# Closing block of a transformer kernel in three passes, and float32 sums for its second norm

## The chip, the cores and the metric
The kernel runs on all eight cores of one Trainium2 chip. Each core computes 1024 of the 8192 tokens (2 batches of 4096) and reads all weights; cores exchange nothing. The metric is the device time of the slowest core in microseconds, and the reported number is the median of the runs. TensorE (PE) multiplies, VectorE (DVE), ScalarE (ACT) and GpSimd (POOL) do the elementwise work, and SyncE (SP), ACT and POOL each can issue DMA transfers on a queue of their own.

## What is computed
```python
h = rmsnorm(x, g_mix)
proj = h @ w_in                                  # 2048 -> u | v | z, 1024 each
u, v = gelu(proj[:, :1024]), gelu(proj[:, 1024:2048])
out_a = spatial_gating(u, v, w_s, b_s, g_v)      # per chunk of 128 tokens
out_b = multiscale_pool(z, w_pool, pool_scale)
x = x + concat(out_a, out_b) @ w_out             # 2048 -> 2048
h = rmsnorm(x, g_ffn)                            # the second norm
x = x + square(relu(h @ w_up)) @ w_down          # 2048 -> 8192 -> 2048
return rmsnorm(x, g_final)                       # the final norm
```
`rmsnorm(x, g)` is x divided by the root of the mean of its squares over 2048 channels, times g.

## The kernel before
Channels lie on partitions and tokens in the free dimension, so 2048 channels are 16 tiles of 128 partitions by 1024 tokens (`XR(m)` is tile m of the residual, float32, in `xr_h` or `xr_mid`). A product has weights of 128x128 as the stationary operand and 512 tokens as the moving one. One "job" (`pe_job`) is the sum over 16 input tiles k for one output tile m: 32 matmuls for both halves of the tokens, or 16 for one half. Results go into six PSUM banks in rotation (`NRING`); banks 6 and 7 hold the statistics.

The norm's factor needs a sum over all channels, hence over partitions. It is made on TensorE: the squares of a tile in bfloat16 (`sqr`) are multiplied by a 128x128 matrix of ones and summed over the 16 tiles in bank 6 or 7. ACT then makes `rstd_bc`, the reciprocal root, by Ln and Exp.

Weights are float32 in HBM. POOL's queue loads them, cast to bfloat16, as slabs of two output tiles (1 MB of float32) into a ring of five slots (`ringall`, `issue_loads`); the load of slab n waits for the job that last used slab n-5.

Every engine's instructions are listed in program order with their dependences (`P.add`, `P.dma`), and an engine runs its list strictly in order, waiting on semaphores. So what stands where in each list is what sets the order; there is no planner.

The stages that matter here:

- Output projection (`wo_part`, `wo_evac`, `wo_norm`, from 212 us): 16 tiles m. For each, TensorE runs 32 matmuls (L664), DVE adds the input tile `xstage` (loaded by SP two tiles ahead, into the buffer that evacuation m-2 has freed, L626) to both halves (L671), ACT writes the scaled bfloat16 copy `h2T` (L682) and the squares (L685), and TensorE adds the squares' sums by two matmuls (L693, L694), which stand in its list behind a later tile's job (`pend`, `flush_one`). Those of tiles 14 and 15 come behind the first job of the up projection.
- Feed-forward in four blocks of 2048 hidden channels: 16 up jobs (reading `h2T`, results squared into `MIX`), then 16 down jobs with the residual added by DVE (L803, L805). The fourth block's down jobs are written apart, as the closing block.
- Closing block (L813 to L865): once for each half of 512 tokens, 16 jobs of 16 matmuls. After each job comes the statistic matmul of the tile before (L853), DVE adds the residual (L841), ACT squares (L847) and multiplies by g_final in place (L857). The second half loads all eight slabs of the block's w_down again. At the end of a half the last tile's statistic, Ln (L862) and Exp (L865) follow. `final_half_out` multiplies by `rstd_bc` on DVE (L819) and stores one tile of 128x512 from SP's queue (L821): for the first half one tile behind each job of the second, for the second half all 16 at the end.

Of the kernel before, what the change touches and what calls it, by code (L numbers as in the profile page):

```python
# [24 lines left out]
NFB = DFF // (FB * 128)  # L25

# [62 lines left out]
def build_program(debug=False):  # L89
# [23 lines left out]
    out_d = nc.dram_tensor("outT", [D, TOK], F32, kind="ExternalOutput").ap()  # L113
# [9 lines left out]
    def sb(name, shape, dt, off):  # L123
        return nc.alloc_sbuf_tensor_at(name, list(shape), dt, offset=off)
# [24 lines left out]
    wstg = sb("wstg", [128, KC // 4, 4, 512], F32, S0)  # L149
    ringall = sb("ringall", [128, 2 * NSLOT, KC, 128], BF16, R0)  # L150

    gv_t = calloc("gv_t", [128, 1024], F32, 4096)
    rtmp = sb("rtmp", [128, 2, 512], F32, C0)
    bs_t = calloc("bs_t", [128, 1024], F32, 4096)
    rstd_bc = calloc("rstd_bc", [128, TOK], F32, 4096)
    wpool = calloc("wpool", [128, 4, 2, 256], BF16, 4096)
    wsT = calloc("wsT", [128, 8, 128], BF16, 2048)
# [477 lines left out]
    pend = []  # L635
    rexp2 = [None, None]
# [40 lines left out]
    def wo_norm(m):  # L677
        while len(pend) > 1:
            flush_one()
        parts = [(0, 512, x1_e[0][m]), (512, 1024, x1_e[1][m])] if m == KC - 1 else [(0, 1024, x1_e[1][m])]  # L680
        for c0, c1, ev in parts:
            h2h[1][m] = P.add("act", lambda e, c0=c0, c1=c1: e.activation(out=h2T[:, m, c0:c1], in_=XR(m)[:, c0:c1], func=AF.Copy,  # L682
                                                                        scale=vecs[:, G_FFN + m:G_FFN + m + 1]), [ev, mix_tile_last[7], cst])
        s = m % 2
        sq = P.add("act", lambda e: e.activation(out=sqr[:, s, :], in_=XR(m)[:, :], func=AF.Square), [x1_e[1][m], hs_reader[2 * s + 1]])  # L685

        def mk():
            d = [sq, ones_op]
# [65 lines left out]
    for fb in range(NFB):  # L754
        act_ops = [None] * FB
        lastblk = fb == NFB - 1
        for f in range(FB):
# [17 lines left out]
            for half in range(2):  # L775
# [4 lines left out]
                    [job, r2[0], rt_readers[s], vh_ops[7]])  # L780
# [32 lines left out]
    fb = NFB - 1  # L813
    pre_ops = [[None] * KC, [None] * KC]
    rexp = [None, None]

    def final_half_out(k, half):
        c0, c1 = half * 512, (half + 1) * 512
        o = P.add("dve", lambda e: e.tensor_tensor(out=XR(k)[:, c0:c1], in0=XR(k)[:, c0:c1], in1=rstd_bc[:, c0:c1], op=ALU.mult),  # L819
                  [rexp[half], pre_ops[half][k]])  # L820
        P.dma("sp", lambda e: e.dma_start(out=out_d[k * 128:(k + 1) * 128, c0:c1], in_=XR(k)[:, c0:c1]), "st", [o])  # L821

    for half in range(2):
        c0, c1 = half * 512, (half + 1) * 512
        pending = [None]
        last_mm = None
        for m in range(KC):
            n, mmi = nbase + fb * 16 + 8 + half * 8 + m // 2, m % 2
            if mmi == 0:
                issue_loads(n + NSLOT - 1)  # L830
            if half == 0 and m == 0:
                segs = [([(0, 0, 512, RS(n, k, mmi * 128, (mmi + 1) * 128), MIX(k)[:, c0:c1], k == 0, k == FB - 1)], [slab_ld[n], act_ops[k]])
                        for k in range(FB)]
            else:
                segs = [([(0, 0, 512, RS(n, k, mmi * 128, (mmi + 1) * 128), MIX(k)[:, c0:c1], k == 0, k == FB - 1) for k in range(FB)],
                         [slab_ld[n], act_ops[FB - 1]])]
            job, banks = pe_job(segs, nb=1)
            slab_done[n] = job
            if pending[0] is not None:
                last_mm = pending[0]()  # L840
            ev = P.add("dve", lambda e, m=m, b=banks[0], c0=c0, c1=c1: e.tensor_tensor(out=XR(m)[:, c0:c1], in0=XR(m)[:, c0:c1], in1=ps[:, b, :], op=ALU.add),  # L841
                       [job, x2_ops[m], x2_e1[m], h2_ops[m]])
            bank_last[banks[0]] = ev
            hsl = hs_ctr[0] % 4
            hs_ctr[0] += 1
            sq_ap = sqr[:, hsl // 2, (hsl % 2) * 512:(hsl % 2) * 512 + 512]
            sq = P.add("act", lambda e, m=m, sq_ap=sq_ap, c0=c0, c1=c1: e.activation(out=sq_ap, in_=XR(m)[:, c0:c1], func=AF.Square), [ev, hs_reader[hsl]])  # L847

            def mk(m=m, sq=sq, sq_ap=sq_ap, hsl=hsl, half=half):
                d = [sq, ones_op]  # L850
                if m == 0:
                    d.append(bank_last[6 + half])
                pe = P.add("pe", lambda e: e.matmul(ps[:, 6 + half, :], ones[:, :], sq_ap, start=(m == 0), stop=(m == KC - 1)), d)  # L853
                hs_reader[hsl] = pe
                return pe
            pending[0] = mk
            pre_ops[half][m] = P.add("act", lambda e, m=m, c0=c0, c1=c1: e.activation(out=XR(m)[:, c0:c1], in_=XR(m)[:, c0:c1], func=AF.Copy,  # L857
                                                                                      scale=vecs[:, G_FIN + m:G_FIN + m + 1]), [ev, sq, cst])
            if half == 1:
                final_half_out(m, 0)  # L860
        last_mm = pending[0]()
        ln = P.add("act", lambda e, half=half, c0=c0, c1=c1: e.activation(out=rstd_bc[:, c0:c1], in_=ps[:, 6 + half, :], func=AF.Ln, bias=EPSB, scale=1.0 / D),  # L862
                   [last_mm, eps_op, last_rstd_reader[0]])
        bank_last[6 + half] = ln
        rexp[half] = P.add("act", lambda e, c0=c0, c1=c1: e.activation(out=rstd_bc[:, c0:c1], in_=rstd_bc[:, c0:c1], func=AF.Exp, scale=-0.5), [ln])  # L865
    for k in range(KC):
        final_half_out(k, 1)

    keys = P.finalize()
    with ExitStack() as es:  # L870
# [19 lines left out]
        @block.sync  # L890
        def _(e):
            P.emit("sp", e, sems)
            e.wait_ge(sems["dma_st"], P.dma_counts["dma_st"])
    return nc
# [60 lines left out]
```

How the kernel before makes its waits and increments, by code:

```python
    def emit(self, eng, e, sems):  # L72
        waited = {}
        for op in self.ops[eng]:
            for d in op.deps:
                if d.kind == "c" and d.eng == eng and eng in ("pe", "sp"):
                    continue
                assert d.val is not None
                if waited.get(d.semkey, 0) >= d.val:
                    continue
                e.wait_ge(sems[d.semkey], d.val)
                waited[d.semkey] = d.val
            ins = op.fn(e)
            if op.kind == "d":
                ins.then_inc(sems[op.semkey], 16)
            elif op.signal:
                ins.then_inc(sems[eng], 1)
# [802 lines left out]
        @block.sync  # L890
        def _(e):
            P.emit("sp", e, sems)
            e.wait_ge(sems["dma_st"], P.dma_counts["dma_st"])
```

## Time and profile before

| | us |
|---|---|
| median of 3 runs (lowest, highest) | 1246.85 (1245.58, 1465.36) |
| profiled run, its time | 1246.34 |
| profiled run, span of its slowest core (core 7) | 1244.8 |
| spans of the eight cores in it | 1238.2 to 1244.8 |

The highest of the three is a run in which a die ran at a lower clock. The page of the profile and all rows are of core 7 in the profiled run. Times are microseconds from the span's start unless marked ns. A record of a matmul lasts from its start until its result is drained, so neighbours overlap; what counts in a stream is the distance from start to start.

### The profile page before, as it was taken

How to read it: one execution, taken by the hardware profiler on the slowest of the kernel's cores; microseconds unless marked ns; L12 is line 12 of the kernel's file. 1: busy time of each engine (PE TensorE's matmuls, PEld its weight loads, DVE VectorE, ACT ScalarE, POOL GpSimd, SP SyncE). 2: the span in 40 equal slices, each digit the busy share in tenths (PEclk: the TensorE clock that was granted, in tenths of full speed). 3: DMA queues.
4: the chain of work that ended last, by engine and by line, in shares of the span. 5: the costliest groups of instructions: out<-in, count | busy, mean ns of one | idle time of the engine just before them, and what ended most of it. 6: DMA issues, size and time to landing. Idle time of an engine off the chain costs nothing.

```text
span 1244.8 us, 14345 instructions; the slowest of 8 cores (1238.2 to 1244.8 us)
## 1 busy us (share of the span) xinstructions
PE 1202.4 (97%) x5736; PEld 547.2 (44%) x5736; DVE 334.8 (27%) x551; ACT 230.6 (19%) x443; POOL 82.0 (7%) x113
## 2 busy tenths in 40 slices
PE   4899999999999999999999999999999999999993
PEld 2354444444444444444444444444444444444441
DVE  3466556321122121212111111111111111121234
ACT  2401155133321100001110000111100011123332
POOL 0100022100000000000000000000000000001000
PEclk9999999999999999999999999999999999999997
DMA  8994530987534443444345433443454335458875
GB/s 277 232 173 76 85 77 2 160 176 156 118 68 70 86 81 69 69 88 80 68 70 88 80 68 71 88 79 68 70 90 77 68 69 94 76 93 144 147 158 169
DMA packets 37921, 126.95 MB, mean 102 GB/s; under 512 B 2784, under 2 KB 2912, under 8 KB 36832
## 3 DMA queue, kind: packets, MB, share of 16 engines
q0 software_dynamic: 24912, 95.43, 45.1%
q1 hardware_dynamic: 12944, 30.61, 7.7%
q8 instruction: 47, 0.77, 0.2%
q14 instruction: 18, 0.15, 0.0%
HBM read 213.05 MB, written 8.39 MB: 178 GB/s over the span
## 4 chain that ended last, share of the span: by engine, by line
PE 93%; DMA 4%; DVE 1%; SPq 1%; ACT 0%; issue 0%; DVEq 0%; ACTq 0%
PE ps L219 83%; PE ps L664 7%; DMA xf<-xT 2%; DMA xstage<-xT 2%; PE ps L407 1%; PE ps L853 1%; SPq L237 0%; PE ps L319 0%; DVE xr_h L819 0%; DVE xr_mid L819 0%; PE ps L541 0%; PE ps L358 0%; PE ps L693 0%; PE ps L694 0%; SPq L241 0%
## 5 line engine op out<-in xcount | busy, mean ns | idle before, releaser
L219 PE MATMUL ps<-h2T,ringall 128*128 128x512 bf16 x2048 | 442.8, 379 | 0.0
L219 PEld LDWEIGHTS ps<-h2T,ringall 128*128 128x128 bf16 x2048 | 200.4, 98 | 241.6
L219 PE MATMUL ps<-pooled,ringall 128*128 128x512 bf16 x1024 | 234.1, 379 | 0.0
L219 PE MATMUL ps<-uT,ringall 128*128 128x512 bf16 x1024 | 234.1, 379 | 0.0
L778 DVE SCALAR_TENSOR_TENSOR rtmp<-ps,rstd_bc 128x512 f32<-128x512 f32 x128 | 82.4, 686 | 360.9 <-PE ps L219 350.0
L219 PEld LDWEIGHTS ps<-pooled,ringall 128*128 128x128 bf16 x1024 | 100.2, 98 | 120.8
L219 PEld LDWEIGHTS ps<-uT,ringall 128*128 128x128 bf16 x1024 | 100.1, 98 | 120.7
L783 ACT ACTIVATE uT<-rtmp 128x512 bf16<-128x512 f32 x64 | 39.1, 631 | 504.6 <-DVE rtmp L778 504.4
L219 PE MATMUL ps<-hT,ringall 128*128 128x512 bf16 x384 | 83.7, 379 | 0.0
L783 ACT ACTIVATE pooled<-rtmp 128x512 bf16<-128x512 f32 x64 | 39.3, 631 | 181.7 <-DVE rtmp L778 181.7
L284 POOL DMA_DIRECT2D ringall<-w_down x40 | 28.6, 714 | 454.1 <-PE ps L219 379.9
L219 PEld LDWEIGHTS ps<-hT,ringall 128*128 128x128 bf16 x384 | 37.3, 98 | 44.4
L219 PE MATMUL ps<-ringall,hT 128*128 128x512 bf16 x256 | 56.2, 379 | 0.0
L803 DVE TENSOR_TENSOR xr_mid<-xr_mid,ps 128x512 f32<-128x512 f32 x24 | 16.5, 687 | 134.9 <-PE ps L219 134.9
L803 DVE TENSOR_TENSOR xr_h<-xr_h,ps 128x512 f32<-128x512 f32 x24 | 16.5, 687 | 134.9 <-PE ps L219 134.9
L284 POOL DMA_DIRECT2D ringall<-w_up x32 | 22.8, 713 | 425.9 <-PE ps L219 340.5
L664 PE MATMUL ps<-uT,ringall 128*128 128x512 bf16 x224 | 50.6, 379 | 0.2 <-DVE uT L549 0.2
L664 PE MATMUL ps<-pooled,ringall 128*128 128x512 bf16 x224 | 50.6, 379 | 0.0
L407 PE MATMUL ps<-hT,ringall 128*128 128x512 bf16 x128 | 37.0, 416 | 0.8 <-ACT hT L386 0.8
L219 PEld LDWEIGHTS ps<-ringall,hT 128*128 128x128 bf16 x256 | 24.8, 98 | 29.0
L664 PEld LDWEIGHTS ps<-uT,ringall 128*128 128x128 bf16 x224 | 21.8, 98 | 26.9 <-issue 0.7
L664 PEld LDWEIGHTS ps<-pooled,ringall 128*128 128x128 bf16 x224 | 21.8, 98 | 26.0 <-issue 0.2
(103 smaller groups left out, 541.5 us busy)
## 6 DMA issues: line engine op xcount, KB each, us to landing
ringall<-w_down POOLq DMA_DIRECT2D x40, 1024.0 KB, 9.5
ringall<-w_up POOLq DMA_DIRECT2D x32, 1024.0 KB, 9.5
ringall<-w_in POOLq DMA_DIRECT2D x10, 1024.0 KB, 11.6
xf<-xT SPq DMA_DIRECT2D x8, 1024.0 KB, 19.7
xstage<-xT SPq DMA_DIRECT2D x16, 512.0 KB, 10.5
ringall<-w_out POOLq DMA_DIRECT2D x7, 1024.0 KB, 16.9
wstg<-w_in SPq DMA_DIRECT2D x4, 1024.0 KB, 15.8
outT<-xr_h SPq DMA_DIRECT2D x16, 256.0 KB, 3.9
```

Of the source, the lines that this page charges most:

```text
L219: ins = e.matmul(ps[:, banks[sel], c0:c1], lhsT, rhs, start=st, stop=sp_)
L284: slab_ld[n] = P.dma("pool", lambda e, n=n: e.dma_start(out=ringall[:, 2 * (n % NSLOT):2 * (n % NSLOT) + 2, :, :], in_=slabs[n]), "slot%d" ...
L407: ins = e.matmul(ps[:, z_banks[half][m], :], ringall[:, m, k, :], hT[:, k, half * 512:(half + 1) * 512], start=(k == 0), stop=(k == KC - 1))
L664: ins = e.matmul(ps[:, banks[half], :], wo_w(m, k), MIX(k)[:, half * 512:(half + 1) * 512], start=(k == K_POOL[0]), stop=(k == K_GATE[-1]))
L778: a1 = P.add("dve", lambda e, s=s, half=half, b=banks[half]: e.scalar_tensor_tensor(out=rtmp[:, s, :], in0=ps[:, b, :], scalar=0.0, in1=rs ...
L783: a2 = P.add("act", lambda e, s=s, f=f, half=half: e.activation(out=MIX(f)[:, half * 512:(half + 1) * 512], in_=rtmp[:, s, :], func=AF.Squ ...
L803: e1 = P.add("dve", lambda e, m=m, b=banks[0]: e.tensor_tensor(out=XR(m)[:, 0:512], in0=XR(m)[:, 0:512], in1=ps[:, b, :], op=ALU.add), [jo ...
L853: pe = P.add("pe", lambda e: e.matmul(ps[:, 6 + half, :], ones[:, :], sq_ap, start=(m == 0), stop=(m == KC - 1)), d)
```

## The change
The output projection: squares of tile 0 go as float32 into `sqacc`, those of tiles 1 to 13 into the one buffer `sqf`, and DVE adds `sqf` to `sqacc`, one tile behind (`accumulate`). After tile 13 DVE splits the sum into two bfloat16 parts, high and low, which TensorE multiplies by the ones (4 matmuls). Tiles 14 and 15 keep direct squares (`sq_end`) and two matmuls each.

The closing block: `PASSES` are tokens 0 to 512, 512 to 768 and 768 to 1024. The weights are loaded once: ten tiles stay in the ring's five slots and six go into `wres`, in the place of `h2T`, with loads that wait for the last up job. The tiles of passes 0 and 1 are multiplied by g_final and `rstd_bc` in one DVE operation and stored from SP during the next pass. The last pass keeps ACT's product with g_final. At its end DVE multiplies 12 tiles and POOL 4, in groups of 1, 1, 2, 4, 4 and of 2, 2, into `ostage`; DVE reads the reciprocal root from PSUM, POOL from SBUF, for which Exp runs twice. The groups are stored from SP's and ACT's queues in seven transfers. The output tensor has a new shape, 128 partitions of 16384 floats, which the host puts in order.

```diff
+PASSES = ((0, 512), (512, 768), (768, 1024))
+NRES = 6
-    out_d = nc.dram_tensor("outT", [D, TOK], F32, kind="ExternalOutput").ap()
+    out_d = nc.dram_tensor("outT", [128, KC * TOK], F32, kind="ExternalOutput").ap()
...
-        for j in range(8):
+        for j in range(8 if fb < NFB - 1 else NSLOT):
             slabs.append(w_down_d[:, 16 * fb + 2 * j:16 * fb + 2 * j + 2, :, :])
-    for j in range(8):
-        slabs.append(w_down_d[:, 16 * (NFB - 1) + 2 * j:16 * (NFB - 1) + 2 * j + 2, :, :])
...
+        if sq_wait:
+            accumulate(sq_wait.pop())
+        first, direct = m == 0, m >= SQ_DIRECT          # SQ_DIRECT = KC - 2
+        dst = sqacc if first else sq_end[m - SQ_DIRECT] if direct else sqf
+        sq = P.add("act", lambda e: e.activation(out=dst[:, :], in_=XR(m)[:, :], func=AF.Square), [x1_e[1][m], acc_last[0]])
...
+    def accumulate(item):
+        m, sq = item
+        acc_last[0] = P.add("dve", lambda e: e.tensor_tensor(out=sqacc[:, :], in0=sqacc[:, :], in1=sqf[:, :], op=ALU.add), [sq, acc_last[0]])
+        if m == SQ_DIRECT - 1:
+            hi = P.add("dve", lambda e: e.tensor_copy(out=sqr[:, 0, :], in_=sqacc[:, :]), [acc_last[0]] + hs_reader)
+            lo = P.add("dve", lambda e: e.tensor_tensor(out=sqr[:, 1, :], in0=sqacc[:, :], in1=sqr[:, 0, :], op=ALU.subtract), [hi])
...
+    issue_loads(NSLAB - 1)
+    up_last = slab_done[nlast - 1]
+    for j in range(NRES // 2):
+        t0 = 16 * NFB - NRES + 2 * j
+        wres_ld.append(P.dma("pool", lambda e, j=j, t0=t0: e.dma_start(out=wres[:, 2 * j:2 * j + 2, :, :], in_=w_down_d[:, t0:t0 + 2, :, :]),
+                             "wres%d" % j, [up_last]))
...
+    def final_out(i, k):
+        t0, t1 = PASSES[i]
+        o = P.add("dve", lambda e: e.scalar_tensor_tensor(out=XR(k)[:, t0:t1], in0=XR(k)[:, t0:t1], scalar=vecs[:, G_FIN + k:G_FIN + k + 1],
+                                                          in1=rstd_bc[:, t0:t1], op0=ALU.mult, op1=ALU.mult), [rexp[i], x3_ops[i][k], cst])
+        P.dma("sp", lambda e: e.dma_start(out=out_block(i, k, 1), in_=XR(k)[:, t0:t1]), "st", [o])
+    for i, (t0, t1) in enumerate(PASSES):
...
+            if i > 0:
+                final_out(i - 1, m)
...
+    for eng, m0, n in (("dve", 0, 1), ("dve", 1, 1), ("pool", lo0, 2), ("dve", 2, 2), ("dve", 4, 4), ("pool", lo0 + 2, 2), ("dve", 8, 4)):
+        rs = rps if eng == "dve" else rstd_bc[:, t0:t1]
+        tail_ops[m0] = (n, P.add(eng, lambda e, m0=m0, n=n, rs=rs: e.tensor_tensor(
+            out=ostage[:, m0:m0 + n, :], in0=xr_group(m0, n), in1=rs.unsqueeze(1).broadcast_to([128, n, T]), op=ALU.mult),
+            [exp_ps if eng == "dve" else rexp[-1], pre_ops[m0 + n - 1], last_job]))
+    for queue, sem, starts in (("sp", "st", (0, 2, 8)), ("act", "sta", (1, lo0, 4, lo0 + 2))):
+        for m0 in starts:
+            n, o = tail_ops[m0]
+            P.dma(queue, lambda e, m0=m0, n=n: e.dma_start(out=out_block(len(PASSES) - 1, m0, n), in_=ostage[:, m0:m0 + n, :]), sem, [o])
```

## Rows read from the trace of the kernel before

**Rows 1.** The page: its span, and the chain that ended last by engine

```profile
span 1244.8 us, 14345 instructions; the slowest of 8 cores (1238.2 to 1244.8 us)
...
PE 93%; DMA 4%; DVE 1%; SPq 1%; ACT 0%; issue 0%; DVEq 0%; ACTq 0%
```

**Rows 2.** Windows: window, length, busy us (instructions) by engine, PEclk, DMA share, GB/s

```profile
205.00:258.00 53.00, 51.81 (x258) 23.99 (x257) 20.67 (x42) 14.96 (x44) 8.24 (x10) 1.00 0.71 126
...
331.00:1105.30 774.30, 774.30 (x3590) 351.00 (x3588) 143.87 (x224) 83.28 (x134) 39.97 (x56) 1.00 0.44 77
...
1165.70:1224.30 58.60, 58.60 (x272) 26.45 (x271) 19.36 (x31) 21.99 (x33) 2.14 (x3) 1.00 0.65 139
```

**Rows 3.** The same view, a stretch within the output projection

```profile
250.00:255.00 5.00, 5.00 (x25) 2.24 (x23) 1.29 (x2) 0.18 (x1) 0.00 (x0) 1.00 1.00 186
```

**Rows 4.** Timeline (start, length, instruction): statistics at both halves' ends, first product

```profile
1163.55 0.38 PE L853 MATMUL ps<-sqr,ones 128*128 128x512 bf16 x1
...
1165.50 0.38 PE L853 MATMUL ps<-sqr,ones 128*128 128x512 bf16 x1 [1.57 <-ACT sqr L847]
...
1224.01 0.38 PE L853 MATMUL ps<-sqr,ones 128*128 128x512 bf16 x1
...
1227.96 2.49 DVE L819 TENSOR_TENSOR xr_h<-xr_h,rstd_bc 128x512 f32<-128x512 f32 x4 [2.39 <-ACT rstd_bc L865]
```

**Rows 5.** Transfers: two windows and the stores of the end; the first 35 us

```profile
1232.00:1238.00 6.00, 0.00 (x0) 0.00 (x0) 5.68 (x10) 0.00 (x0) 0.00 (x0) 0.50 1.08 287
1238.00:1241.00 3.00, 0.00 (x0) 0.00 (x0) 0.00 (x0) 0.00 (x0) 0.00 (x0) 0.50 1.06 368
...
L821 SPq DMA_DIRECT2D outT<-xr_h x8: 332/560/977, 1228.7 to 1238.7; - x8
...
DMA to landing us min/median/max: 2.9/5.0/5.9
...
DMA packets 3296, 9.93 MB, mean 284 GB/s; under 512 B 444, under 2 KB 572, under 8 KB 2620
```

**Rows 6.** Chain by time (start, us): matmuls of 16 and 128 columns, two projection tiles

```profile
75.77 0.79 PE ps L358 x32
...
186.12 0.45 PE ps L541 x8
...
301.68 6.91 PE ps L664 x32
309.02 6.91 PE ps L664 x32
```

**Rows 7.** Timeline of the output projection's first half, PE and DVE

```profile
233.92 0.38 PE L693 MATMUL ps<-sqr,ones 128*128 128x512 bf16 x1
...
253.43 1.29 DVE L671 TENSOR_TENSOR xr_h<-ps,xstage 128x512 f32<-128x512 f32 x2 [8.16 <-DMA xstage<-xT]
...
257.06 0.38 PE L693 MATMUL ps<-sqr,ones 128*128 128x512 bf16 x1 [0.96 <-ACT sqr L685]
...
260.14 1.29 DVE L671 TENSOR_TENSOR xr_mid<-ps,xstage 128x512 f32<-128x512 f32 x2 [5.42 <-DMA xstage<-xT]
```

**Rows 8.** Groups by form (busy us, mean ns of one): durations used for new operations

```profile
L841 DVE TENSOR_TENSOR xr_h<-xr_h,ps 128x512 f32<-128x512 f32 x16 | 11.0, 687 | 44.1 <-PE ps L219 44.1
...
L847 ACT ACTIVATE sqr<-xr_h 128x512 bf16<-128x512 f32 x16 | 10.1, 631 | 35.7 <-DVE xr_h L841 35.7
...
L603 ACT ACTIVATE sqv<-vf 128x128 f32<-128x128 f32 x64 | 18.8, 299 | 0.4
...
L433 DVE TENSOR_TENSOR tmpA<-zE 128x1039 f32<-128x1039 f32 x8 | 9.9, 1232 | 0.1
...
L605 POOL TENSOR_SCALAR vrs<-vstat 128x8 f32<-128x8 f32 x8 | 2.5, 318 | 50.5 <-ACT sqv L603 50.5
...
L446 DVE TENSOR_TENSOR ptmp<-tmpA,invc 128x16 f32<-128x16 f32 x4 | 0.7, 175 | 0.4
...
L415 DVE TENSOR_TENSOR sqh<-xh 128x256 bf16<-128x256 f32 x1 | 0.4, 418 | 0.0
```

More of the change, by code:

```diff
@@ new lines, in stat_sum, with fn, mk @@
+    def stat_sum(parts, start, stop, deps):
+        def fn(e):
+            ins = None
+            for i, p in enumerate(parts):
+                for half in range(2):
+                    ins = e.matmul(ps[:, 6 + half, :], ones[:, :], p[:, half * 512:(half + 1) * 512], start=start and i == 0, stop=stop)
+            return ins
+        return P.add("pe", fn, deps)
+    def accumulate(item):
[4 more added lines that the diff above has]
+            lo = P.add("dve", lambda e: e.tensor_tensor(out=sqr[:, 1, :], in0=sqacc[:, :], in1=sqr[:, 0, :], op=ALU.subtract), [hi])
+            def mk():
+                pe = stat_sum([sqr[:, 0, :], sqr[:, 1, :]], True, False, [hi, lo, ones_op, bank_last[6], bank_last[7]])
+                hs_reader[:] = [pe] * 4
+                return pe, m
+            pend.append(mk)
@@ L811, in build_program @@
         prev_down_last = dj
[L813 to L824, printed above, removed]
+    nlast = nbase + (NFB - 1) * 16 + 8
@@ L850, in mk @@
+            sq = P.add("act", lambda e, m=m, sq_ap=sq_ap, t0=t0, t1=t1: e.activation(out=sq_ap, in_=XR(m)[:, t0:t1], func=AF.Square), [ev, hs_reader[hsl]])
+            def mk(m=m, sq=sq, sq_ap=sq_ap, hsl=hsl, T=T, sbank=sbank):
                 d = [sq, ones_op]
                 if m == 0:
-                    d.append(bank_last[6 + half])
-                pe = P.add("pe", lambda e: e.matmul(ps[:, 6 + half, :], ones[:, :], sq_ap, start=(m == 0), stop=(m == KC - 1)), d)
+                    d.append(bank_last[sbank])
+                pe = P.add("pe", lambda e: e.matmul(ps[:, sbank, 0:T], ones[:, :], sq_ap, start=(m == 0), stop=(m == KC - 1)), d)
@@ L856, in build_program @@
             pending[0] = mk
[L857 to L860, printed above, removed]
+            if lastp:
+                pre_ops[m] = P.add("act", lambda e, m=m, t0=t0, t1=t1: e.activation(out=XR(m)[:, t0:t1], in_=XR(m)[:, t0:t1], func=AF.Copy,
+                                                                                    scale=vecs[:, G_FIN + m:G_FIN + m + 1]), [ev, sq, cst])
@@ L865, in build_program @@
-        rexp[half] = P.add("act", lambda e, c0=c0, c1=c1: e.activation(out=rstd_bc[:, c0:c1], in_=rstd_bc[:, c0:c1], func=AF.Exp, scale=-0.5), [ln])
-    for k in range(KC):
-        final_half_out(k, 1)
+        bank_last[sbank] = ln
+        if lastp:
+            rps = ps[:, 7, 0:T]
+            exp_ps = P.add("act", lambda e, t0=t0, t1=t1: e.activation(out=rps, in_=rstd_bc[:, t0:t1], func=AF.Exp, scale=-0.5), [ln, bank_last[7]])
+        rexp[i] = P.add("act", lambda e, t0=t0, t1=t1: e.activation(out=rstd_bc[:, t0:t1], in_=rstd_bc[:, t0:t1], func=AF.Exp, scale=-0.5), [ln])
@@ L952 @@
         b, q = divmod(c, 4)
-        out[b, q * TOK:(q + 1) * TOK, :] = np.asarray(res.results[c]["outT"], np.float32).T
+        o = np.asarray(res.results[c]["outT"], np.float32)
+        for t0, t1 in PASSES:
+            blk = o[:, KC * t0:KC * t1].reshape(128, KC, t1 - t0)
+            out[b, q * TOK + t0:q * TOK + t1, :] = blk.transpose(2, 1, 0).reshape(t1 - t0, D)
     return out
```

80 lines of the change are left out of this document (48 added, 32 removed).

## The prediction

> **What bounds the kernel now.** I read the shares of the chain that ended last first: 93% of the 1244.8 us span are TensorE's [rows 1]. Then the stages in windows [rows 2]. In the feed-forward stages (331 to 1105 us) TensorE has no idle time at a granted clock of 1.00, the 2.4 GHz level, and the same holds in the second half of the closing block. Shortening anything there pays only if it takes matmuls out of TensorE's queue. Two stretches differ. One is the first half of the output projection (205 to 258 us), where TensorE idles 1.19 us [rows 2] while the DMA engines are full [rows 3]. The other is the end: the last projection matmuls end near 1224.0, and the span ends at 1244.8. These 20.8 us hold a short chain of ACT and DVE work and then stores [rows 4, 5]. The change touches exactly these: the statistic matmuls of the output projection, the closing block and the end.
>
> **Part A, the second norm's sums.** Before, each of 16 tiles costs two 512-column matmuls with the ones (L693, L694), 32 in all. Matmuls start 6.91/32 = 0.216 us apart [rows 6], and from the tile at 301.68 to that at 309.02 the period is 7.34 us: 32 projection matmuls (6.91) and one pair (0.43) [rows 6]. After, the split sum takes 4 matmuls and tiles 14 and 15 take 2 each: 8 in all. 24 x 0.216 = 5.2 us leave TensorE's queue, and nothing takes their place: the pairs that are left sit after tile 15 and after the first up tile.
> The new work lies on DVE and ACT. Thirteen float32 additions of 1024 columns (nearest row 1.23 us, L433), a cast and a subtraction (1.23 each at most) [rows 8] add 1.3 us per 6.9 us tile to the 1.3 of the two evacuations. ACT's next square waits for the addition, and that ends about as ACT's own scaled copy of the tile does (1024 columns, twice a 512-column row of 0.63 at most). I cost this at nothing; its cover is TensorE's 6.9 us tile, of which some 4 us stay free. If that cover failed, a tile would cost at most the 1.23 us of one addition more. The addition stands in DVE's queue ahead of later evacuations, hence of freed banks, but those come a tile later.
> One stall also goes. The pair of tile 3 waited 0.96 us for its square, because the input tile for it had landed only at 253.4 [rows 7]. What is late next: six banks in pairs, so job m needs the evacuation of m-3. Without pairs and stall, jobs 3, 4, 5 run from 233.92 to 254.65 (3 x 6.91), and job 6 needs evacuation 3, over at 254.72 [rows 7]: a start near 254.8 instead of 257.5, right behind the pair at 257.06. Job 7 is then ready at 261.7, and evacuation 4 is over at 260.14 + 1.29 = 261.4. That is 0.3 us of room; later tiles have 3 us. So the stall is worth 0.96 - 0.15 = 0.8 us, and A is 5.2 + 0.8, taken as 5.9 us. The lower bound is the case in which nothing is gained ahead of job 6, because the DMA engines set its time (share 1.00 from 250 to 255 [rows 3]): after job 6 there were 24 of the 32 matmuls and now 8, so 16 x 0.216 = 3.45 us. The upper bound is 6.1.
>
> **Part B, the closing block.** Pass 0 is the former first half, with the same matmuls. Passes 1 and 2 have 2 x 272 matmuls of 256 columns, where the second half had 272 of 512. No row has 256 columns. Spacings are 0.79/32 = 25 ns at 16 columns, 0.45/8 = 56 at 128 and 216 at 512 [rows 6]; all three with their own weight load, whose record lasts 98 ns (0.10 us in the timelines). Were it not hidden, 207 ns each would cost 53 us; at 25 and 56 ns it is hidden. They lie on columns/2.4 plus 2.5 ns down to 128 columns, so 256 columns cost 109 ns; bounds are 108 (half of 216) and 112 (twice 56). 542 x 0.109 = 59.2 against 271 x 0.216 = 58.5: +0.7 us, bounds 0.0 to 2.2.
> As a check on this, the Trainium skill, "TensorE: Matmul & The Clock Gate", section on the back-to-back issue gap, gives sustained spacings of 81 ns at 128 and 131 ns at 512 columns with a weight load each. The trace disagrees on both (56 and 216). An estimate between its figures would be 98 ns at 256 columns, 5 to 6 us less for the block than my sum; I go by the rows.
> There is one more pass boundary. At the present one, statistic 15 starts 1.95 us after statistic 14 (1163.55 to 1165.50): drain, evacuation, square [rows 4]. With 256 columns the evacuation goes from 0.69 to 0.42 us and the square from 0.63 to 0.41 (between the rows of 128 and 512 columns, and a DVE row of 256, L415 [rows 8]): 1.95 - 0.49 = 1.46 us, say 1.4. The rest of it, some 1.3 us beyond the matmul itself, is new idle time, bounds 1.0 to 1.9. Within a pass, the same chain of 1.4 us must fit under one job of 16 x 0.109 = 1.75 us, and does. On DVE evacuation and the previous pass's final multiplication take 0.35 + 0.61 of 1.86 us. That is cover, but thin: if the chain grew by 0.4 us, each further 0.1 us would cost 3.2 us over 32 tiles.
> Weights are loaded once: 5 slots and 3 loads into the dead h2T, 8 loads instead of the 16 of the code before. On POOL's queue the last four stand behind the last up tile and nothing waits behind them. The first is needed 8 x 3.67 = 29 us later; 4.2 MB at the 186 GB/s of a full stretch [rows 3] take 23. I cost it at nothing (if it were late, up to 3 us once). The two-operand final multiplication replaces an ACT copy and a DVE product, off the path. SP issues 32 stores in the passes, one in 1.86 us, where one takes 0.33 [rows 5]. B: -0.7 - 1.4 - 0.2 for a shorter cover at the first job of each pass = -2.3 us, range -1.0 to -4.
>
> **Part C, the end.** Before, from 1224.01 to DVE's first product at 1227.96 there are 3.95 us [rows 4]. With 256 columns: evacuation -0.27, square -0.22, statistic -0.11, Ln -0.22, Exp -0.22: about -1.0 us.
> From the first product (call it D) to the end there were 16.8 us [rows 4]. DVE made 256 KB in 0.61 us, 430 GB/s, and the DMA engines were full (share 1.08 and 1.06) at 287 and 368 GB/s [rows 5]. So stores set this end. The two full windows together give (6 x 287 + 3 x 368)/9 = 314 GB/s; 4.19 MB take 13.3 us at that, and the other 3.5 us are the first product and issue ahead and the landing behind. After, only 2.10 MB are left: 6.7 us, and the first product is 0.35 us shorter. Does the supply keep up? DVE: 0.33, 0.33, 0.60, 1.14, 1.14 = 3.6 us for 12 tiles (PSUM as an operand costs the same: 0.69 us in L841 [rows 8]; four products from SBUF alone take 3 x 0.61 + 0.68 = 2.5 [rows 4]). POOL multiplies 4 tiles in two operations that no row shows; the same shape on DVE takes 0.69, and POOL's smallest operation takes 318 ns where a small one on DVE takes 175 (L446) [rows 8], 1.8 times, so 0.7 to 1.24 us each. All is supplied by D+3.8, while DMA needs until about D+8. So D+6.7+3.5-0.35 = D+9.9, and at the 368 GB/s of the better window D+8.8. I take 9.6, since two of seven groups are twice and two four times as wide as a store before, so -7.2 us. Issues on ACT have no row; SP's took 0.33 to 0.98, and four in 3 us fit. C: 8.2 us; bounds 3.8 (below) and 9.0 (368 GB/s all the time).
>
> **Sum.** 5.9 - 2.3 + 8.2 = 11.8 us. Span 1244.8 - 11.8 = 1233.0; the profiled run took 1.5 us more than its span (1246.34), and the median 1246.85 lies 0.5 above that: 1235.
>
> **Rivals.**
> Input tiles set the projection. The weight load now issued at 254 instead of 256.65 competes with input tile 4; A falls to 3.45 and the time is 1237.5. For it: DMA is full there. Against: the 3 us of room from tile 5 on.
> The end is bound by supply and landing. DVE and POOL hold each other up in SBUF, so the products last 3.6 + 2.5 = 6.1 us, and the last 512 KB land like the slowest 256 KB did (5.9 us [rows 5]) plus 2: D+14, a gain of 2.8 instead of 7.2: 1239.4. Against: DVE's rstd now comes from PSUM.
> Stores in the new layout are slow (the other side). The output now has partitions 64 KB apart, in pieces of 1 to 4 KB, instead of rows 4 KB apart. Ahead of D 4.6 us are saved, so the end may take 21.4 us; less 3.2 that is 2.10 MB in 18.2 us: below 115 GB/s the kernel gets slower. At 100 it takes 21 us for them, 1250, and more with the backlog of pass 1. Against: loads of xT have the same 64 KB step, and the opening moved 9.93 MB at 284 GB/s with them [rows 5]. Beside it, the Trainium skill, "DMA: Bandwidth & Descriptors", section on latency and other measured facts, reports copies between tensors in HBM falling from 207 to 103 GB/s as the partitions' step grows from 512 KB to 4 MB. No run here shows it.
> Narrow matmuls run closer than 109 ns. If what spaces them were the weight load's 98 ns, 542 x 0.011 = 6.0 us less: 1229. The straight line through three rows speaks against.
> The change doesn't shorten TensorE's queue, the pairs of statistics being free already: then A is 0.8 and the time 1240. The 7.34 us period speaks against.
>
> **Chances.** Forecast 0.62; input tiles 0.13; supply and landing 0.14; slow stores 0.03; closer matmuls 0.04; statistics free 0.02; else 0.02. The range 1230 to 1242 takes in the first three and the bounds of B, with two rivals together. About 2% (25 us) is what a measurement of this kernel can tell from no change: faster than that 0.02, within it 0.94, slower 0.04 (slow stores far below 100 GB/s, or the thin cover in the narrow passes gone).
>
> **What the profile would show.** Right: the tile period in the projection is 6.91 instead of 7.34 and there are 8 statistic matmuls there; 16 matmuls of 256 columns take 1.75 us; two idle gaps of 1.6 and 1.3 us in the closing block; 8 loads of w_down in it; the end from the last projection matmul takes 12 to 13 us (2.95 + 9.6) instead of 20.8, with DMA share near 1 for most of it. Wrong: TensorE idle at each tile of a narrow pass; a bank wait of over 1 us at jobs 6 to 9; stores under 200 GB/s at the end; POOL's products over 2 us.

## The result, and the profile after

| | before | after |
|---|---|---|
| median (lowest, highest), us | 1247.06 (1245.58, 1465.36), 4 runs | 1236.84 (1234.72, 1238.04), 4 runs |
| profiled run, us | 1246.34 | 1238.04 |
| its span, slowest core | 1244.8 (core 7) | 1236.2 (core 0) |
| spans of all cores | 1238.2 to 1244.8 | 1229.5 to 1236.2 |

The execution of 1465.36 had one die at a lower clock; the ratios, and the medians in the sections below, leave such executions out. The ratio is 0.9917, with an interval from 0.9903 to 0.9931: some 10 us faster, well inside 2%, against a forecast of 1235. The total came out close; on the slowest cores two of its three terms did not, and their errors cancel. The page of the kernel after, its span, transfers and chain by engine (before: [rows 1]):

```profile
span 1236.2 us, 14873 instructions; the slowest of 8 cores (1229.5 to 1236.2 us)
...
DMA packets 36755, 118.59 MB, mean 96 GB/s; under 512 B 2768, under 2 KB 5200, under 8 KB 35664
...
PE 92%; DMA 5%; DVE 1%; issue 1%; SPq 1%; ACT 0%; DVEq 0%; ACTq 0%
```

DMA's share of the chain rose from 4% to 5% although the end, where the stores stand, got shorter. Two waits for input tiles stand in the output projection. The first, for tile 3, was in the chain before too, with 21.84 us; the second, for tile 5, is new. This is the chain in order of time (start, length, step), kernel after:

```profile
231.50 22.28 DMA xstage<-xT
255.23 15.59 DMA xstage<-xT
```

**Where the time went.** Four marks split the span. The end of the projection is read at the start of the second up job, since all statistics of the second norm stand ahead of it. The other marks are the statistic of tile 14 in pass 0, the one of tile 14 in the last pass, and the first product of the end, D.

| us, slowest core | before | after | change | forecast |
|---|---|---|---|---|
| second up job starts (A) | 338.64 | 337.92 | -0.7 | -5.9 |
| statistic 14, pass 0 | 1163.55 | 1162.83 | -0.7 | |
| from there to statistic 14, last pass (B) | 60.46 | 62.64 | +2.2 | +2.3 |
| statistic 14 to D (C) | 3.95 | 2.82 | -1.1 | -1.0 |
| D to the end (C) | 16.84 | 7.91 | -8.9 | -7.2 |
| span | 1244.8 | 1236.2 | -8.6 | -11.8 |

These are marks of core 7 before and of core 0 after. On average over the eight cores of the same two traces the span fell by 9.0 us: A gave 2.7, B cost 2.2, and C gave 1.1 and 7.3 (from D to the end 15.4 before, 8.1 after). Core 7 had the longest end of the eight before (14.7 to 16.8 us). So C's gain beyond the forecast is one of the slowest cores; on average only A missed.

The closing block and the end, timeline of the kernel after (start, length, instruction, idle time before it):

```profile
1162.83 0.38 PE L896 MATMUL ps<-sqr,ones 128*128 128x512 bf16 x1
...
1164.78 0.38 PE L896 MATMUL ps<-sqr,ones 128*128 128x512 bf16 x1 [1.57 <-ACT sqr L890]
...
1194.47 0.27 PE L896 MATMUL ps<-sqr,ones 128*128 128x256 bf16 x1
...
1195.87 0.27 PE L896 MATMUL ps<-sqr,ones 128*128 128x256 bf16 x1 [1.13 <-ACT sqr L890]
...
1225.47 0.27 PE L896 MATMUL ps<-sqr,ones 128*128 128x256 bf16 x1
...
1228.29 1.35 DVE L925 TENSOR_TENSOR ostage<-xr_h,ps 128x256 f32<-128x256 f32 x3 [1.74 <-ACT ps L911]
1228.74 2.48 POOL L925 TENSOR_TENSOR ostage<-xr_h,rstd_bc 128x512 f32<-128x512 f32 x2 [120.60 <-ACT rstd_bc L912]
```

The wide boundary is the old one (1.95 us, as in [rows 4]); the narrow one takes 1.40. Windows inside the two narrow passes, and in the last stores (columns as in [rows 2]):

```profile
1164.90:1194.40 29.50, 29.50 (x271) 26.43 (x271) 16.34 (x30) 7.58 (x17) 0.00 (x0) 1.00 0.34 126
1195.90:1225.40 29.50, 29.50 (x271) 26.42 (x272) 12.24 (x30) 14.71 (x32) 0.00 (x0) 1.00 0.21 72
...
1230.00:1233.00 3.00, 0.00 (x0) 0.00 (x0) 1.90 (x2) 0.00 (x0) 1.22 (x1) 0.50 0.98 366
```

TensorE has no idle time in either pass: the thin cover held. The stores flow at 366 GB/s, where the old end had windows of 287 and 368 [rows 5].

**Why A gave so little here.** The projection of the kernel after on core 0, timeline:

```profile
255.31 3.61 PE L672 MATMUL ps<-pooled,ringall 128*128 128x512 bf16 x16 [0.51 <-DVE xr_h L679]
255.35 0.72 POOL L289 DMA_DIRECT2D ringall<-w_out  x1 [23.45 <-PE ps L672]
...
261.77 1.29 DVE L679 TENSOR_TENSOR xr_mid<-ps,xstage 128x512 f32<-128x512 f32 x2 [5.48 <-DMA xstage<-xT]
...
263.21 3.61 PE L672 MATMUL ps<-pooled,ringall 128*128 128x512 bf16 x15 [0.83 <-DVE xr_mid L679]
...
270.91 1.29 DVE L679 TENSOR_TENSOR xr_mid<-ps,xstage 128x512 f32<-128x512 f32 x2 [6.72 <-DMA xstage<-xT]
...
272.35 2.97 PE L672 MATMUL ps<-pooled,ringall 128*128 128x512 bf16 x7 [2.07 <-DVE xr_mid L679]
```

Jobs 6, 7 and 8 each wait for a freed bank: 0.51, 0.83 and 2.07 us, together 3.41. The evacuations that free the banks wait for input tiles. Tile 5's load was issued at 255.23, the load of 1 MB of w_out at 255.35, and the tile took 15.59 us to land, to 270.8. In the kernel before, the same two marks are these (core 7):

```profile
256.65 0.71 POOL L284 DMA_DIRECT2D ringall<-w_out  x1 [24.75 <-PE ps L664]
...
263.87 1.29 DVE L671 TENSOR_TENSOR xr_mid<-ps,xstage 128x512 f32<-128x512 f32 x2 [2.43 <-DMA xstage<-xT]
```

There the weight load was issued at 256.65, and evacuation 5 began at 263.87, not 270.91. What follows the third wait, in windows of the same core:

```profile
270.00:272.00 2.00, 0.27 (x2) 0.00 (x0) 1.09 (x2) 0.00 (x0) 0.72 (x1) 1.00 0.17 62
272.00:274.00 2.00, 1.65 (x5) 0.72 (x6) 2.00 (x4) 1.71 (x2) 0.00 (x0) 0.64 0.21 20
274.00:276.00 2.00, 2.00 (x7) 0.64 (x5) 1.76 (x2) 1.66 (x3) 0.00 (x0) 0.51 0.95 168
276.00:278.00 2.00, 2.00 (x11) 0.94 (x10) 0.00 (x0) 1.03 (x1) 0.00 (x0) 1.00 1.01 161
```

The granted clock fell to the 1.2 GHz level (7 matmuls in 2 us where 9 or 10 fit) and came back. That costs 0.36 x 2 + 0.49 x 2 = 1.7 us. So 3.4 + 1.7 = 5.1 us of A's 5.9 are taken back on this core. The others waited less: over the eight cores, the second up job starts at 336.87 on average before and at 334.16 after, 2.7 us earlier.

That start also holds what came before the projection. The projection's first matmul is at 208.18 to 211.92 us on the eight cores before and at 210.03 to 212.13 after. From there to the second up job the stage takes 126.46 us on average before and 123.03 after, 3.4 less. The four kernels under "The end" leave this stage alone, and in their traces it takes 121.8 to 122.4 on average, 4.1 to 4.6 less. So A's yield differs from execution to execution, and that of the profiled one here is the lowest of these five.

### The profile page after: what moved, and what is told of

Read it like the earlier page. It is cut to its first block, busy times and chain, and to the rows that moved or that the text cites. A ratio compares the mean times of both kernels' runs of the same rounds, so it can differ in the third digit from the quotient of the medians.

```text
span 1236.2 us, 14873 instructions; the slowest of 8 cores (1229.5 to 1236.2 us)
## 1 busy us (share of the span) xinstructions
PE 1193.5 (97%) x5880; PEld 571.5 (46%) x5984; DVE 354.9 (29%) x587; ACT 221.0 (18%) x446; POOL 78.8 (6%) x107
## 4 chain that ended last, share of the span: by engine, by line
PE 92%; DMA 5%; DVE 1%; issue 1%; SPq 1%; ACT 0%; DVEq 0%; ACTq 0%
PE ps L226 83%; PE ps L672 6%; DMA xstage<-xT 3%; DMA xf<-xT 2%; PE ps L412 1%; PE ps L896 1%; SPq L244 0%; PE ps L324 0%; PE ps L546 0%; DVE ostage L925 0%; PE ps L363 0%; SPq L248 0%; DVE xr_h L679 0%; PE ps L709 0%; DVE xr_h L883 0%
## 5 line engine op out<-in xcount | busy, mean ns | idle before, releaser
L226 PE MATMUL ps<-pooled,ringall 128*128 128x512 bf16 (+1 forms) x989 | 212.1, 362 | 1.0
L226 PE MATMUL ps<-uT,ringall 128*128 128x512 bf16 (+1 forms) x992 | 212.1, 362 | 0.8
L226 PE MATMUL ps<-hT,ringall 128*128 128x512 bf16 x375 | 82.6, 379 | 0.6 <-issue 0.2
L672 PE MATMUL ps<-pooled,ringall 128*128 128x512 bf16 x218 | 51.7, 388 | 3.7 <-DVE xr_mid L679 2.9
L672 PE MATMUL ps<-uT,ringall 128*128 128x512 bf16 x220 | 50.4, 379 | 0.4 <-DVE uT L554 0.2
L289 POOL DMA_DIRECT2D ringall<-w_down x29 | 20.7, 714 | 379.9 <-PE ps L226 379.9
L412 PE MATMUL ps<-hT,ringall 128*128 128x512 bf16 x125 | 35.4, 409 | 0.8 <-ACT hT L391 0.8
```

Of the source, the lines that this page charges most:

```text
L226: ins = e.matmul(ps[:, banks[sel], c0:c1], lhsT, rhs, start=st, stop=sp_)
L289: slab_ld[n] = P.dma("pool", lambda e, n=n: e.dma_start(out=ringall[:, 2 * (n % NSLOT):2 * (n % NSLOT) + 2, :, :], in_=slabs[n]), "slot%d" ...
L412: ins = e.matmul(ps[:, z_banks[half][m], :], ringall[:, m, k, :], hT[:, k, half * 512:(half + 1) * 512], start=(k == 0), stop=(k == KC - 1))
L672: ins = e.matmul(ps[:, banks[half], :], wo_w(m, k), MIX(k)[:, half * 512:(half + 1) * 512], start=(k == K_POOL[0]), stop=(k == K_GATE[-1]))
```

## The experiments

Theory 1 throughout: the new sums take 5.2 us out of TensorE's queue, as forecast, but the stage then asks for input tiles earlier, beside a weight load that is issued earlier too, and the tiles come late; the end is a matter of store bytes and their rate. Its rivals stand in the expectations. Where these speak of the "last statistic" of the projection: in kernels with the new sums it is one row of four matmuls, 0.87 us ahead of the second up job, in the others a row of one, 0.21 ahead. That makes the new sums look 0.66 us better than they are, so I compare starts of the second up job ("U", all eight cores). U includes where the projection began, which differs by up to 4 us between the cores of a trace; where that matters I give the stage's length, from its first matmul to U.

### The two halves of the change alone

The first kernel is the one before with `accumulate`, `sq_end` and the split sum, the second is the one after with pairs of statistics for each tile again:

```diff
 # sums only, on the kernel before
-        s = m % 2
-        sq = P.add("act", ... out=sqr[:, s, :] ...)        # two matmuls per tile
+        first, direct = m == 0, m >= SQ_DIRECT
+        dst = sqacc if first else sq_end[m - SQ_DIRECT] if direct else sqf
 # block only, on the kernel after: the same lines the other way round
```

> The kernel before with only the new sums of the second norm's squares (part A); closing block and output as before. Theory 1 (the sums take 24 matmuls out of TensorE's queue, but the output projection is then held by its input tiles: they still arrive from full DMA queues, and jobs 6, 7 and 8 wait for freed banks): the start of the up projection moves 2 to 3 us earlier in the mean of the cores and about 1 us on the slowest; time 1243.5 to 1246, ratio 0.997 to 0.999; bank waits of 1 to 4 us per core between 250 and 275 us. Theory 2 (the forecast: TensorE alone sets the projection): 5 to 6 us less, time near 1241, ratio 0.995, bank waits under 0.5 us.

> The changed kernel with the old sums of the second norm (parts B and C alone). Theory 1 (the end gained 10 us on the slowest core, the block lost 2.2, and part A gave little): time 1238.5 to 1240, ratio 0.993 to 0.995; from the first product to the end about 8 us. Theory 2 (part A gave its 5 us and the end only about 8): time near 1241, ratio 0.9955.

Sums only: 1243.65 us (from 1241.10 to 1248.39) beside 1246.26, ratio 0.9983 (0.9967 to 0.9999). U is 334.63 on average (329.7 to 338.1), 2.2 us better than before. Waits of TensorE on core 6 (total, times, longest):

```profile
PE ps L670 <- DVE xr_mid L677: 3.1, 1, 3.1
PE ps L877 <- ACT sqr L871: 3.1, 2, 1.6
PE ps L670 <- DVE xr_h L677: 1.0, 1, 1.0
```

The bank waits are there without the block: they come with the new sums. Block only: 1241.34, ratio 0.9956 (0.9939 to 0.9972), where 1238.5 to 1240 was expected. Its last stage does what theory 1 says: D to the end takes 7.81 to 8.18 us on all cores. But U is 338.10 on average (335.4 to 342.1), 1.2 us later than before, for work that is the same in both. The stage began no later (210.4 on average in both), so the 1.2 us are inside it. The waits of its core 7, the slowest (total, times, longest):

```profile
PE ps L695 <- ACT sqr L687: 3.0, 1, 3.0
```

Input tile 4 took 17.23 us to land there, its square came 2.98 us late for the statistic matmuls at 266.18, and the granted clock then fell as above (0.91 from 262 to 280 us). So tiles can come late with the old sums too; TensorE then waits for a square and not for a bank. The longest such wait in the kernel before was 1.61 us, on core 4. This stage moves by a microsecond or two between kernels with the same instructions in it.

### Weight loads held back

`issue_loads` makes a slab's load wait for an input tile as well:

```diff
+    late_for = {17: 5, 18: 7}     # slab: input tile
 ...
+            if n in late_for:
+                deps.append(xs_ld[late_for[n]])
```

> The changed kernel with two waits more on POOL's queue: the w_out loads of tiles 12, 13 and of 14, 15 start only when input tiles 5 and 7 have landed; they are needed 30 us later. Theory 1 (the moved-up w_out load shares the DMA engines with input tiles 4, 5, 6, and that makes jobs 6 to 8 wait; on two cores the wait of 2.1 us also drops TensorE's clock to 1.2 GHz for 4 us): waits of TensorE between 250 and 275 us fall under 1 us per core, granted clock 1.00 in the stage on all cores, time 2 to 4 us below the changed kernel, 1232.5 to 1235. Theory 2 (the input tiles are late for another reason, their own double buffer and the four earlier weight loads): waits stay, time as the changed kernel, 1236 to 1237.

> The changed kernel with the w_out loads of tiles 8 to 15 issued one by one, each after an input tile has landed (after tiles 3, 4, 6 and 8), so that input tiles 2 to 6 meet at most one weight load. Theory 1 (input tiles late because DMA is shared with five weight loads): input tile 2 is added before 240 instead of 245.5, no bank waits, TensorE without idle time from 230 to 330 us; time 3 to 5 us below the changed kernel, 1231.5 to 1234. Theory 2 (TensorE's queue is not what the projection waits for, or the delayed weights come late themselves): no gain, or new waits of TensorE for w_out loads; 1236 or more.

The second kernel has {15: 3, 16: 4, 17: 6, 18: 8} and also lists these four loads one by one, with tiles 3, 4, 6 and 7, so that each can wait for its own input tile. With the first, no core waits for a bank between 250 and 275 us, the clock stays at 1.00 there, and U is 329.2 to 331.8 on six cores. Their stage takes 120.2 to 120.4 us, some 6 less than before. That is the forecast of A, by an edit that touches only when weights are loaded: the cause is shown. Yet the time is 1237.23, ratio 0.9931 (0.9916 to 0.9945), no better than after, where 1232.5 to 1235 was expected. Two cores have a new wait; core 0 of it, timeline:

```profile
321.82 1.29 DVE L682 TENSOR_TENSOR xr_h<-ps,xstage 128x512 f32<-128x512 f32 x2 [5.68 <-DMA xstage<-xT]
323.03 1.21 DVE L718 TENSOR_TENSOR sqacc<-sqacc,sqf 128x1024 f32<-128x1024 f32 x1
324.35 0.69 DVE L720 CAST sqr<-sqacc 128x1024 bf16<-128x1024 f32 x1
325.14 1.23 DVE L721 TENSOR_TENSOR sqr<-sqacc,sqr 128x1024 bf16<-128x1024 f32 x1
...
326.52 1.39 PE L712 MATMUL ps<-sqr,ones 128*128 128x512 bf16 x4 [4.03 <-DVE sqr L721]
```

Input tile 14 landed at 321.8. The loads behind the delayed ones had bunched up (DMA share 0.96 from 284 to 320 us); that this made it late is what the next experiment tries. The addition, cast and subtraction stand behind its evacuation in DVE's queue, and the four matmuls stand ahead of the whole up projection: 4.0 us idle, and U is 336.8 there. The granted clock falls here too (0.76 from 326 to 333 us), which takes another 1.7 us. With {15: 3, ...} it is the same at other cores: no bank waits, 3.2 and 5.0 us at the split sum on cores 1 and 5, 1237.17 us, ratio 0.9917 (0.9893 to 0.9942), where 1231.5 to 1234 was expected. The gain was made and given back 60 us later.

### All weight loads of the stage held back

```diff
-    late_for = {17: 5, 18: 7}
+    late_for = {17: 5, 18: 7, 19: 9, 20: 11, 21: 13, 22: 15}
 # and, in the second kernel, the split sum's matmuls behind the first up job
-        while len(pend) > 1:
+        while len(pend) > 1 and m < KC - 1:
```

> The changed kernel with the two delayed w_out loads of e3_late_weights and also the four w_up loads of the projection held back, each until input tile 9, 11, 13 or 15 has landed (they are needed 13 to 50 us later). Theory 1 (the whole projection runs close to what the DMA engines can bring, some 18 MB in 110 us at 180 GB/s, and which input tile is late depends on what shares the engines with it): no TensorE wait over 1 us on any core, neither at 250 to 275 nor at 320 to 330, all cores end the stage within 3 us; time 1231 to 1234. Theory 2 (the late tiles 13 and 14 of two cores in e3_late_weights come from the delay of the two w_out loads, so more delay is worse): waits of 3 us and more at the end of the stage, or TensorE waits for w_up in the first up jobs; 1236 or more.

> As e5_all_late, and the four matmuls of the split sum stand behind the first up job instead of ahead of it. Theory 1 (in TensorE's queue they wait for DVE's evacuation of tile 14, hence for input tile 14, and block an up job that could run): on cores where tile 14 is late the 3 to 5 us of waiting in front of the up job shrink to under 1.5 us; where it isn't late nothing changes; time 1231 to 1233, with less spread than e5_all_late. Theory 2 (the up job needs the tile too, so the wait only moves into it): as e5_all_late within 0.5 us.

1232.21 us beside 1245.55, ratio 0.9888 (0.9873 to 0.9903). U is 331.42 on average (329.1 to 333.1): 5.5 us ahead of before, although the stage began 0.6 us later. Its length is 120.43 on average, 6.0 less than before, where the forecast for A was 5.9, and 120.2 to 120.6 on all eight cores. Core 1 of it, the last of the eight there, its waits in that stage (a single one), and one window over the stage:

```profile
PE ps L675 <- DVE uT L558: 0.2, 1, 0.2
```

```profile
205.00:330.00 125.00, 124.76 (x603) 57.34 (x601) 53.40 (x81) 42.07 (x69) 11.81 (x15) 1.00 0.71 146
```

0.24 us idle in 125, clock 1.00. The stage is bound by TensorE's queue alone, and moving as many bytes as before (DMA share 0.71) was never the obstacle; their order was. The second kernel gives 1232.37, the same ratio: with no tile late, the place of the four matmuls decides nothing, so this run doesn't settle what it would be worth in the kernels above.

The same six waits on the kernel before:

> The kernel before with nothing but the held-back weight loads of e5_all_late (two of w_out, four of w_up). Theory 1 (the old sums leave TensorE 5.2 us more to do in the projection, so its input tiles were hardly late; only the wait of 0.3 to 2.1 us for a square goes): 0.5 to 2 us less, ratio 0.9985 to 0.9995, and the last statistic of the stage at 335.5 to 337 on all cores. Theory 2 (holding back the weights is a gain of its own, whatever the sums): 4 us less, ratio near 0.9965.

1242.56 beside 1243.52, ratio 0.9992 (0.9981 to 1.0002), U 334.94 on average (333.5 to 337.0, where 335.5 to 337 was expected for the statistic 0.2 us ahead of it). By the time it is worth nothing that can be told; of the 1.9 us in U, 1.2 are an earlier start of the stage. The late weights pay because the sums shortened the stage, not by themselves. The stage's length shows it: on average 126.46 us before, 124.11 with the sums alone, 125.74 with the late loads alone and 120.43 with both (the kernel above), that is 2.3 and 0.7 us for each and 6.0 together. The last core's U says the same: 339.15, 338.14, 337.02 and 333.09.

### The end

All stores from SP; one transfer a tile; the output tensor in its former shape:

```diff
-    for queue, sem, starts in (("sp", "st", (0, 2, 8)), ("act", "sta", (1, lo0, 4, lo0 + 2))):
+    for queue, sem, starts in (("sp", "st", (0, 1, 2, lo0, 4, lo0 + 2, 8)),):        # one queue
-            P.dma(queue, ... out_block(..., m0, n), in_=ostage[:, m0:m0 + n, :])
+            for j in range(n):                                                        # single tiles
+                P.dma(queue, ... out_block(..., m0 + j, 1), in_=ostage[:, m0 + j:m0 + j + 1, :])
-        return out_d[:, KC * t0 + k0 * (t1 - t0):KC * t0 + (k0 + nk) * (t1 - t0)]
+        return out_d[:, k0:k0 + nk, t0:t1]                                            # old layout
```

> The changed kernel with the seven last stores all issued from SP. Theory 1 (the end was shortened by halving what is left to store; 2.1 MB at 375 GB/s keep the DMA engines full for 5.6 of its 7.9 us, and seven issues of 0.33 us fit on one queue): from the first product to the end 7.7 to 8.3 us, as before. Theory 2 (the second queue feeds the engines better than one): 9 to 10 us.

> The changed kernel with the 16 tiles of the last pass stored one by one (pieces of 1 KB for each partition instead of up to 4 KB), from the same two queues behind the same products. Theory 1 (wide pieces raised the store rate from 314 to 375 GB/s): from the first product to the end 9 to 9.8 us, rate near 300 GB/s with the engines full. Theory 2 (width does not matter; the rate of before was low because half as wide a window of queues or the cores' shares set it): 7.7 to 8.3 us.

> The changed kernel with the old output tensor (a partition's rows 4 KB apart), passes and groups kept; a group's transfer then has pieces of 1 KB. Theory 1 (the width of pieces matters, the distance of partitions does not): as t2_single_tiles, 9 to 9.8 us from the first product to the end. Theory 2 (the new 64 KB distance costs something): below t2_single_tiles, 8 us. Theory 3 (neither matters): 7.7 to 8.3 us in both.

These are single executions, so I read D to the end on all eight cores and not the totals (1236.48, 1235.79 and 1238.56 us).

| | D to the end, us | GB/s, D + 1.7 to D + 4.7 |
|---|---|---|
| after | 7.91 to 8.40 | 365 to 370 |
| one queue | 7.74 to 7.94 | 363 to 370 |
| single tiles | 8.44 to 8.59 | 318 to 320 |
| old layout | 8.58 to 8.82 | 312 to 314 |

The same window of single tiles and of one queue:

```profile
1227.30:1230.30 3.00, 0.00 (x0) 0.00 (x0) 1.98 (x2) 0.00 (x0) 1.31 (x2) 0.50 0.95 318
```

```profile
1228.90:1231.90 3.00, 0.00 (x0) 0.00 (x0) 1.87 (x2) 0.00 (x0) 1.20 (x1) 0.50 0.98 369
```

The second queue is worth nothing. The Trainium skill, "DMA: Bandwidth & Descriptors", in its rules for kernel authors, says that spreading transfers over several issuing engines gives no bandwidth, since all use the same 16 DMA engines; the trace agrees (363 to 370 GB/s either way). The length of the contiguous piece is what the new layout brings: with 1 KB to a partition in each piece, in either layout, 312 to 320 GB/s; with up to 4 KB 365 to 370. It is worth 0.5 us here, less than I expected (9 to 9.8 us for single tiles), and the 64 KB from partition to partition cost nothing.

Passes of 512, 320 and 192:

```diff
-PASSES = ((0, 512), (512, 768), (768, 1024))
+PASSES = ((0, 512), (512, 832), (832, 1024))
```

> The changed kernel with passes of 512, 320 and 192 tokens. Theory 1 (the end is 2.3 us fixed plus bytes at 375 GB/s, and a job of 192 columns, 16 x 0.0825 = 1.32 us, still covers the chain of evacuation and square, about 1.25): 16 jobs of the last pass in 22.4 us without idle time between them, from the first product to the end 6.5 us instead of 7.9, time 1.5 to 2 us below the changed kernel. Theory 2 (the chain no longer fits under the job): TensorE waits 0.1 to 0.3 us at each statistic, 1.6 to 4.8 us in all, and the gain at the end is lost.

D to the end takes 6.45 to 6.55 us, 1.4 less than after, and statistic 14 to D 2.57 instead of 2.82. The window at the end has the same rate on fewer bytes:

```profile
1226.50:1229.50 3.00, 0.00 (x0) 0.00 (x0) 1.12 (x2) 0.00 (x0) 0.65 (x1) 0.50 1.00 364
```

1.57 MB at 364 GB/s are 4.3 us, and 2.2 us lie around them, as after (2.10 MB at 367 are 5.7, of 7.9). A tile's period is 1.40 us in the last pass, with no wait inside it. So the step is worth 1.6 us by its parts. The stretch from U to the end of the span shows them: 896.8 to 896.9 us on its eight cores, 898.2 to 898.8 in the kernel after. The total doesn't show it: 1237.35 us (from 1233.25 to 1240.81), ratio 0.9949 (0.9929 to 0.9969). Its profiled run was the fastest of all, 1233.25; its projection still has the bank waits (U from 329.4 to 334.6), which differ from execution to execution. The others have no trace. In the two slowest of them the last core's span is 1238.9 and 1237.1 us, where the next core's is 1234.1 and 1232.8: a delay of single cores, as the waits of the projection are, but the reason is argued and not shown.

### Everything together

All six late loads, the split sum behind the first up job, and passes of 512, 320, 192:

> e6_sum_behind_up joined with the passes of 512, 320 and 192 tokens. Theory 1 (both gains are in different places and add): 1.5 to 2 us below e6_sum_behind_up, time 1230 to 1231.5, ratio 0.987 to 0.988, with the small spread of e6_sum_behind_up. Theory 2 (the wide spread of t4_last_192 came from its narrower pass and not from the projection): spread of several us here too and no gain.

1229.83 us (from 1229.73) beside 1243.52, ratio 0.9888 (0.9868 to 0.9908), where 0.987 to 0.988 was expected, and spans from 1226.2 to 1227.9: the fastest version, and better than both kernels. No core waits in the projection (U 329.2 to 331.2), and D to the end is 6.46 to 6.88. Against the late loads without the 192 columns the ratio is the same, but the kernel before was 2 us faster on this chip, so the times leave open what the 192 columns add. The traces tell: from U to the end of the span are 896.7 to 897.2 us here and 898.2 to 899.0 in the two kernels with all late loads, on every core. That is the 1.6 us of the kernel above again.

## Why the prediction was right in its total and wrong in its terms

**What bounds.** Right: TensorE's queue and the end, and the end is stores.

**A, -5.9 forecast, -0.7 on the slowest core, -2.7 on average.** Of the removed work every number held: with the tiles on time the stage is 6.0 us shorter. The step that failed is the one that put job 7 at "0.3 us of room; later tiles have 3 us". It took evacuation 4 from the trace before [rows 7], over at 261.4 (it was over at 263.06), and left the landings of tiles 4 and 5 where they had been. I had seen that the weight load moves from 256.65 to about 254 (it went to 255.35) and that DMA was full [rows 3], and named the collision as a rival at tile 4, to be paid with 16 x 0.216. In fact it fell mostly on tile 5 (15.59 us to land), the waits went through three jobs, and they had a price that no term held: the clock after the wait, 1.7 us. The lower bound of 3.45 was thus no bound. The rival's mechanism was real, its chance of 0.13 far too low, and its time of 1237.5 is nearer to 1236.84 (0.7 us) than the forecast is (1.8 us).

**B, +2.3 forecast, +2.2 measured.** 16 matmuls of 256 columns take 1.75 us, 17 with the statistic 1.855, that is 109 ns each; the three old rows on a line gave exactly this. The Trainium skill, "TensorE: Matmul & The Clock Gate", section on the back-to-back issue gap, calls its formula (columns by 2.4, plus 2.5 ns) that of an isolated matmul, and the trace has it in 271 matmuls in a row with a weight load each. The rival built on closer matmuls is out. The narrow boundary took 1.40 us, as said. Of the sum's terms, 0.7 and 1.4 came as forecast (16 jobs take 29.69 and 29.60 us against 58.51); the 0.2 for a shorter cover did not appear. TensorE's three waits for squares sum to 3.8 us, the longest 1.6.

**C, -8.2 forecast, -10.1 measured on the slowest cores, -8.4 on average.** The chain from statistic to D was right (-1.1 for -1.0). The mis-sized term is D to the end: 9.6 forecast, 7.91 measured. The sum said 9.9, of which I took 9.6. Of the 2.0 us between the sum and 7.91, 1.0 is the rate (2.10 MB at 314 GB/s against 367) and 1.0 what lies ahead and behind (3.15 against 2.2). I averaged two windows of the old end and so took its slow one for a property of stores. In the same window behind D the rate is 365 to 370 GB/s on the new end's eight cores, but 286 to 381 on the old end's. The other part is the core: I read the old end on core 7, where it took 16.8 us, and the mean of the eight is 15.4. So the gain of 7.2 is right on average (7.3), but by luck: both ends are some 1.5 us shorter than I had them. Why the old one dipped to 287 wasn't tried. The rival of supply and landing is refuted: POOL's two products took 2.48 us, 1.24 each, the top of my range, with nothing waiting for them.

**The span.** -0.7 + 2.2 - 10.1 = -8.6 us, 1244.8 to 1236.2. The misses, +5.2 and -1.9, and -0.1 in B leave +3.2 on the span (1236.2 against 1233.0) and 3.0 on the profiled run (1238.04 against 1235); the median of four is 1.2 lower. That A's miss did not show more is luck: the range of 1230 to 1242 held for a partly wrong reason.

**The marks set beforehand.** "A bank wait of over 1 us at jobs 6 to 9" was one that would show a wrong step, and it is there at job 8. The period of 6.91 us, the 8 statistic matmuls and the two gaps (1.57 and 1.13 us) are as foretold; the end of 12 to 13 us is not (10.7 in fact).

## What to carry to other kernels

When work is cut from a stage whose DMA engines are full for a stretch, everything that the stage triggers comes earlier: don't carry landing times over from the old trace, but list which transfers now start together, and let bulk weight loads wait for the small tile that is needed first. Follow the repaired transfers to the end of the stage, since the next late tile may hold up something dearer. And check a total that fits by its parts on all cores: here 5 us lost on one core were partly hidden by a better end. Compare a stage by its own length as well as by when it ends: the cores had begun this one up to 4 us apart.

## What the runs showed of the hardware

- **The clock can fall after a short wait in a dense stream.** After one wait of 2.07 us core 0 ran at 0.64 and 0.51 of full clock for two windows of 2 us. From 262 to 280 us the granted clock was 0.91 on eight cores of after, sums only, block only and old layout, each with a wait of 2.1 to 3.1 us there, and 1.00 on one core of the old layout with 2.15.
- **A float32 input tile beside a casting weight load.** 15.59 us from issue to landing at a DMA share of 0.94 (193 GB/s), some 9 when the weight load is issued 1.9 us after it. One core of block only had 17.23 with the weight load issued 10.9 us after it, so the distance between these two alone doesn't set it.
- **The last stores of a core** move 365 to 370 GB/s in pieces of up to 4 KB to a partition, 312 to 320 in pieces of 1 KB. How far the eight cores store at the same time is not known: counted from each core's own start, they reach D some 7 us apart in the kernel after; in the kernel with everything together they do within 1.9 us, at 363 to 365 GB/s.
- **The final multiplication of two operands** (128x512, float32, one from SBUF's `rstd_bc` and one per partition) takes 0.75 us on DVE in the kernel after, where the product with `rstd_bc` alone took 0.68 in the kernel before.
